# Pool mixer: group product on the residual itself with tokens as outputs, norm factor at PSUM eviction, running means as band products

## The reference, cut

```python
def rmsnorm(x, g):
    return x * lax.rsqrt(jnp.mean(x * x, axis=-1, keepdims=True) + NORM_EPS) * g

def pool_mixer(h, w_group, scale):            # h: (1, 528, 1024), groups of 256 channels
    hf = h.reshape(B, L, 4, 256)
    csum = jnp.cumsum(hf, axis=1)
    for g, w in enumerate((2, 4, 8, 16)):     # running mean over the last w tokens
        prev = jnp.pad(csum[:, :L - w, g, :], ((0, 0), (w, 0), (0, 0)))
        means.append((csum[:, :, g, :] - prev) / jnp.minimum(t, w))   # t = 1 .. L
    mixed = jnp.stack(means, axis=2) - hf
    return jnp.einsum('blgc,gcd->blgd', mixed, w_group).reshape(B, L, 1024) * scale

h = h + rmsnorm(f, norm_ffn_post[0])          # end of layer 0; f is the FFN's output
m = pool_mixer(rmsnorm(h, norm_mix_pre[1]), pool_w_group, pool_scale)
h = h + rmsnorm(m, norm_mix_post[1])
f = conv_ffn(rmsnorm(h, norm_ffn_pre[1]), ...)          # layer 1's FFN follows
```

## Time and profile before

| | |
|---|---|
| median of 3 runs | 2167.58 us (2165.72 to 2169.86) |
| the profiled execution, its own time | 2169.56 us |
| its span in the trace | 2167.8 us (1.76 us lie around it) |
| mean granted TensorE clock | 0.969 of full speed |
| PE busy | 2012.0 us (93%) |
| weight loads on PE | 1824.2 us (84%) |
| DVE, ACT, POOL busy | 958.1, 945.6, 870.7 us |

### The profile page before, as it was taken

The page is one execution under the profiler, slowest core; times in us unless marked ns, Lnnn a source line. Parts: engine busy times, 40 slices in busy tenths (PEclk is TensorE's granted clock), DMA queues, the critical chain, the costliest instruction groups (busy, mean ns, idle before and its releaser), DMA issues.

```text
span 2167.8 us, 36602 instructions
## 1 busy us (share of the span) xinstructions
PE 2012.0 (93%) x13518; PEld 1824.2 (84%) x13522; DVE 958.1 (44%) x1823; ACT 945.6 (44%) x1663; POOL 870.7 (40%) x530
## 2 busy tenths in 40 slices
PE   8999889998999999989888989999999479999997
PEld 6887668888877778989788979999998379999996
DVE  6874870227533230257688164334101864334102
ACT  3123762323644342155577355545423355555322
POOL 1444213442434444324433153443443733443443
PEclk7999999999999999989999999999999789999999
DMA  9641012231222333222100112222331003222332
GB/s 351 242 165 39 11 37 96 92 97 40 88 97 78 106 97 107 69 69 88 50 0 0 40 50 97 94 90 87 98 100 66 20 26 101 96 88 86 107 101 75
DMA packets 55529, 186.49 MB, mean 86 GB/s; under 512 B 7056, under 2 KB 10384, under 8 KB 55440
## 3 DMA queue, kind: packets, MB, share of 16 engines
q1 hardware_dynamic: 53600, 183.07, 25.0%
q10 hardware_dynamic: 1840, 2.19, 0.3%
HBM read 183.13 MB, written 2.10 MB: 85 GB/s over the span
## 4 chain that ended last, share of the span: by engine, by line
PE 82%; DVE 11%; ACT 3%; issue 2%; POOL 1%; DVEq 0%; DMA 0%; ACTq 0%; POOLq 0%
PE PS L686 68%; PE PS L895 2%; PE PS L974 2%; PE PS L853 1%; PE PS L928 1%; DVE work L2718 1%; PE PS L809 1%; DVE pool_s L411 1%; PE PS L870 1%; POOL X L1490 1%; DVE ada_acc L2261 1%; DVE small L2412 1%; PE PS L1052 1%; PE PS L1040 1%; PE PS L1327 1%
## 5 line engine op out<-in xcount | busy, mean ns | idle before, releaser
L1375 POOL TENSOR_TENSOR w_lo<-w_raw,w_hi 128x1024 fp32r<-128x1024 f32 x273 | 661.2, 2429 | 956.7 <-ACT w_hi L1568 956.5
L686 PE MATMUL PS<-H_hi,w_lo 128*128 128x256 f32 (+3 forms) x2184 | 596.0, 322 | 62.0 <-POOL H_lo L1530 26.6
L1568 ACT ACTIVATE w_hi<-w_raw 128x1024 fp32r<-128x1024 f32 (+2 forms) x317 | 307.9, 986 | 689.8 <-PE PS L686 642.0
L686 PE MATMUL PS<-H_lo,w_hi 128*128 128x256 f32 (+3 forms) x2184 | 587.7, 318 | 0.0
L686 PE MATMUL PS<-H_hi,w_hi 128*128 128x256 f32 (+3 forms) x2184 | 586.5, 317 | 0.0
L686 PEld LDWEIGHTS PS<-H_hi,w_lo 128*128 128x128 f32 x2184 | 375.5, 193 | 103.8 <-issue 51.4
L686 PEld LDWEIGHTS PS<-H_hi,w_hi 128*128 128x128 f32 x2184 | 376.0, 193 | 26.0
L686 PEld LDWEIGHTS PS<-H_lo,w_hi 128*128 128x128 f32 x2184 | 376.2, 193 | 24.7
L2718 DVE SCALAR_TENSOR_TENSOR work<-PS,vec,work 128x512 f32<-128x512 f32 (+4 forms) x264 | 187.0, 751 | 450.2 <-ACT work L1868 440.6
L686 PE MATMUL PS<-mid_hi,w_lo 128*128 128x256 f32 (+2 forms) x968 | 228.6, 294 | 3.6 <-DVE work L2718 3.6
L686 PE MATMUL PS<-mid_hi,w_hi 128*128 128x256 f32 (+2 forms) x968 | 226.9, 292 | 0.0
(11 more groups left out here) (334 smaller groups left out, 3053.7 us busy)
## 6 DMA issues: line engine op xcount, KB each, us to landing
w_raw<-stream SPq DMA_DIRECT2D x293, 512.0 KB, 3.7
ada_w<-ada SPq DMA_DIRECT2D x48, 512.0 KB, 6.4
X<-xT SPq DMA_DIRECT2D x8, 256.0 KB, 5.8
yT<-X SPq DMA_DIRECT2D x16, 128.0 KB, 1.7
rel_raw<-rel ACTq DMA_DIRECT2D x4, 256.0 KB, 2.6
vec<-vecs ACTq DMA_DIRECT2D x1, 390.0 KB, 3.8
sin_t<-rope ACTq DMA_DIRECT2D x1, 264.0 KB, 3.8
cos_t<-rope ACTq DMA_DIRECT2D x1, 132.0 KB, 2.4
```

Source lines behind the costliest of these rows:

```text
L686: last = pe.matmul(out[:, c0 + a:c0 + b], w, x[:, a:b], start=start and i == 0, stop=stop and i == 2)
L1375: gp.tensor_tensor(w_lo[:, o], w_raw[:, o], w_hi[:, o].bitcast(F32), ALU.subtract)\
L1568: return act_.activation(out, in_, ACT.Copy, scale=scale)
```

## The change

The group product no longer waits for the norm and the running means. By linearity, mean(norm(x) g) W is done as band * (r * (x (gW))), where r is a factor for each token:

- The gain goes into the weights: `upper_pool` on ACT scales the four 128 x 256 pieces of a pool block in place, then rounds it.
- `H_hi` and `H_lo` are made from `X` itself (`round_x` on ACT, `lower_x` on DVE).
- `pool_tiles(s)` on PE has tokens as outputs: 128 (or 16) tokens of `H` are the stationary operand, 256 columns of weights move. Half 0 has three token tiles (16, 128 and 128 tokens), half 1 two: 72 and 48 matmuls.
- `pool_norms(s)` gives the sums of squares for each token on its own partition: 24 and 16 float32 matmuls of 128 columns, where `sum_x_squares("down_b", s)` is dropped. The root (`root_pool`) works on 3 or 2 columns.
- `take_z` on ACT evicts a token tile with the root as a scale for each partition (`z_hi`, 1024 columns), `lower_z` on DVE makes `z_lo` from PSUM and `z_hi`.
- `pool_half(s)` on PE then multiplies `z` with a band matrix (1/w on w diagonals, less the identity) and gives the transposed layout back: 70 matmuls for half 0 (16 of 144, 16 of 128 and 38 of 16 columns) and 48 for half 1 (128, 144 and 16 columns, 16 of each, in part). `make_bands` builds the bands with 25 small DVE instructions after up_b; the band is waited for in ACT's `take_first("down_b")` before its weight splits, and by PE.
- `pooled_dve`, `pooled_gp`, `lower_gp` and `round_pooled` are gone. On POOL the first pool block's `w_lo` stands ahead of the residual's adds.

The diff, cut:

```diff
+POOL_TILES = (((0, META), (META, P), (META + P, P)), ((HALF2, P), (HALF2 + P, P)))
...
+            def pool_tiles(s):
+                first = 3 * s
                 for b in range(2):
...
+                    for i, (t0, tn) in enumerate(POOL_TILES[s], first):
+                        z = z_psum(i)
...
+                        for kk in range(4):
+                            kt = 4 * b + kk
+                            if i == first:
+                                pe.wait_ge(hh_ok[s], KD + kt + 1)
+                            xs = slice(kt * S2 + t0, kt * S2 + t0 + tn)
+                            ws = slice(slot * BLK + kk * 256, slot * BLK + (kk + 1) * 256)
+                            o = b * 512 + kk // 2 * 256
+                            for j, (l, r) in enumerate(((H_lo, w_hi), (H_hi, w_lo), (H_hi, w_hi))):
+                                last = pe.matmul(PS[0:tn, z, o:o + 256], l[:, xs], r[:, ws],
+                                                 start=kk % 2 == 0 and j == 0, stop=kk % 2 == 1 and j == 2)
...
+                    elif b == 0:
+                        sum_squares("down_b", 1)
+            def pool_norms(s):
+                for k in range(KD):
+                    pe.wait_ge(sqx_ok[s], TAIL_N["down_b"] * KD + k + 1)
+                    for i, (t0, _) in enumerate(POOL_TILES[s]):
+                        o = 512 * s + i * P
+                        last = pe.matmul(PS[:, 0, o:o + P], sqp[:, k * S2 + t0:k * S2 + t0 + P], ones[:, :],
+                                         start=k == 0 and i == 0, stop=k == KD - 1, skip_group_check=True)
+                last.then_inc(sum_ok[s], 1)
+            def pool_half(s):
+                pe.wait_ge(band_ok, 1)
+                pe.wait_ge(zl_ok, 5 if s else 3)
+                for m in range(8):
...
+                    g = m // 2
+                    out = PS[:, m % 4, COL2:]
+                    if s == 0:
+                        parts = ((1, META, P, 0, BAND), (2, META + P, P, 0, P), (0, 16, META, 16, 32))
+                    else:
+                        parts = ((2, HALF2, P, P, BAND), (3, HALF2, P, 0, BAND), (4, HALF2 + P, P, 0, P))
+                    for i, (tile, t0, rows_, a, b) in enumerate(parts):
+                        for t in (z_lo, z_hi):
+                            last = pe.matmul(out[:, t0:t0 + b - a], z_tile(t, tile, m)[0:rows_], band(g)[0:rows_, a:b],
+                                             start=i == 0 and t is z_lo, stop=s == 1 and i == 2 and t is z_hi,
+                                             skip_group_check=True)
...
-            sum_x_squares("down_b", 0)
-            sum_squares("down_b", 1)
+            pool_tiles(0)
+            pool_norms(0)
             pool_half(0)
             sum_squares("pool", 0)
-            sum_x_squares("down_b", 1)
+            pool_tiles(1)
+            pool_norms(1)
             sum_x_squares("pool", 0)
             pool_half(1)
             sum_squares("pool", 1)
...
+                if name == "down_b":
+                    act_.wait_ge(band_ok, 1)
                 cnt_["four"] += 1
...
+                for kk in range(4):
+                    w = w_raw[:, slot * BLK + kk * 256:slot * BLK + (kk + 1) * 256]
+                    chain.done(copy(w, w, v1("mix_pre", KD + 4 * b + kk)))
...
+            def take_z(s):
+                act_.wait_ge(rs2_ok[s], 4)
+                for i, (_, tn) in enumerate(POOL_TILES[s], 3 * s):
...
+                    copy(z_tile(z_hi, i)[0:tn], PS[0:tn, z_psum(i), :], zroot(i)[0:tn]).then_inc(zh_ok, 1)
...
-            next_upper("down_b", 0)
-            square_x("down_b", 0)
-            next_upper("down_b", 1)
+            upper_pool(0)
+            upper_pool(1)
+            for k in range(KD):
+                round_x(0, k)
+                if k >= 2:
+                    square_pool(0, k - 2)
+            square_pool(0, 6)
+            square_pool(0, 7)
+            take_half("down_b", 1)
+            root(1, 3)
             next_upper("down_b", 2)
-            take_half("down_b", 1)
-            root(0, 4)
-            root(1, 3)
+            root_pool(0)
+            take_z(0)
             next_upper("down_b", 3)
-            round_pooled(0)
+            for k in range(KD):
+                round_x(1, k)
             take_half("pool", 0, range(0, 4), "pool_scale")
             take_half("pool", 0, range(4, 8), "pool_scale")
             root(0, 5)
-            square_x("down_b", 1)
-            root(1, 4)
+            for k in range(KD):
+                square_pool(1, k)
+            root_pool(1)
             square_x("pool", 0)
-            round_pooled(1)
+            take_z(1)
...
+            def make_bands():
...
+                v.wait_ge(midl_ok, 2 * KF + 1)
...
+                chain.done(v.tensor_copy(ones_of(0)[:, 16:16 + P], ident[:, :]))
+                for g in range(4):
+                    w = POOLS[g]
+                    chain.wait()
+                    chain.done(v.tensor_tensor(ones_of(g + 1)[:, 16:], ones_of(g)[:, 16:],
+                                               ones_of(g)[:, 16 - w // 2:wide - w // 2], ALU.add))
+                    chain.wait()
+                    chain.done(v.scalar_tensor_tensor(band(g), ones_of(g + 1)[:, 16:], 1.0 / w, ones_of(0)[:, 16:],
+                                                      ALU.mult, ALU.subtract))
...
+            def lower_z(s):
+                for i, (_, tn) in enumerate(POOL_TILES[s], 3 * s):
+                    v.wait_ge(zh_ok, i + 1)
+                    v.scalar_tensor_tensor(z_tile(z_lo, i)[0:tn], PS[0:tn, z_psum(i), :], zroot(i)[0:tn],
+                                           z_tile(z_hi, i)[0:tn].bitcast(F32), ALU.mult, ALU.subtract)\
+                        .then_inc(zl_ok, 1)
...
+            make_bands()
             add_four(2)
             root(0, 3)
+            for k in range(KD + 2):
+                if k < KD:
+                    weigh("down_b", 0, "ffn_post", 0, k)
+                if k >= 2:
+                    lower_x(0, k - 2)
...
-            pooled_dve(0)
...
             root(0, 5)
             for k in range(KD):
                 weigh("pool", 0, "mix_post", KD, k)
-            root(1, 4)
-            pooled_dve(1)
-            before_up("pool", "mix_post", KD, KD + len(POOL_DVE), 2 * KD, KD)
+            root_pool(1)
+            lower_z(1)
+            before_up("pool", "mix_post", KD, 2 * KD, 2 * KD, KD)
```

268 lines of the change are left out of this document (124 added, 144 removed).

## The result

The change made the kernel a little slower: 2172.57 us (median of 12 runs) against 2167.88 (12 runs), a ratio of 1.0022 with an interval of 1.0013 to 1.0031. Forecast were 2155.1 and a gain of 12.5; measured is a loss of 4.7 us, and 2172.57 lies above the range's end of 2168.

What follows compares the result with a forecast made beforehand. PE was taken to bound the kernel outside a few stages, the vector engines this stage. First half -0.3 and second -13.85 sum to -14.15; with +1.65 taken back, -12.5, giving 2155.1 us; range 2147 to 2168.

Steps and rivals of the forecast that it cites:

- rival C: z eviction: DVE's `z_lo` contends with POOL and waits it out, +6 us, 2161 in all; chance 0.08.
- Bands: 70 x 0.115 ... of which the first part runs at the half level, +1.9: First half's band products on PE: 8.1 us, plus 1.9 for a first part at the half clock level.
- 0.5 of half clock: Second half's band products on PE: 0.5 us added for the half level, beside 5.5 for 48 products.
- a sum of -14.15: Pool stage, both halves: -0.3 us in the first and -13.85 in the second, before the reserve.
- D: Rival: TensorE's half clock level stretches the stage's tile products, norms and bands; slower, 2171.6 us; chance 0.10.
- B: Rival: short products cost more, the 118 band products 0.18 us rather than 0.115, +7.7, 2162.8; chance 0.12.
- E: Rival: new chain of norms, root, z, bands as long in the second half too, or bands late; 2165 to 2169; chance 0.08.
- The reserve of 1.65: Pool stage, both halves: +1.65 us taken back from the summed gain for waits and the clock.

Runs made afterwards that it cites:

- e12: Changed kernel with all 70 first-half band products moving 256 columns, 38 of them still at 16 rows, no fillers: 2176.84 us, 1.0043 of before.
- e15: Changed kernel with all 70 first-half band products at 128 rows and 256 columns, no fillers: stage 95.19 us, kernel 2169.23 us (one execution).
- e17: Changed kernel with all 118 band products at 128 rows and 256 columns, unread products in all five waits: 2158.16 us, 0.9951 of before.
- e1: Changed kernel with 48 unread 256-column products between the norm sums and the first half's band products: 2170.57 us, 1.0008 of before.
- e4: Changed kernel with 48 unread products ahead of the first half's bands and more in the other five waits: 2165.88 us, 1.0 of before.
- e8: Changed kernel with the 38 first-half band products of 16 rows given 128 rows, left at 16 columns, no fillers: 2169.11 us.

## Why the prediction was wrong

**What held.** What bounds the kernel in this stage was read rightly, and the forecast's times up to z were close. The last tile of `X` was 17.7 us after the stage's start (17.8 forecast), the norms took 5.52 (5.3), and the root and z of the first half 6.0 (6.2). The second half's bands could start 16.0 us after the sums (16.2). DVE and ACT in the changed kernel, where the bands are built, and `z_lo` of both halves:

```profile
1549.18 0.17 DVE L2899 TENSOR_TENSOR lnw_r<-work,lnw_r 128x16 fp32r<-128x16 f32 x1
...
1549.39 2.96 ACT L1556 ACTIVATE w_hi<-w_raw 128x1024 fp32r<-128x1024 f32 x3 [6.68 <-DVE lnw_r L2899]
...
1692.84 3.65 DVE L2926 SCALAR_TENSOR_TENSOR z_lo<-PS,st,z_hi 16x1024 fp32r<-16x1024 f32 x3 [1.25 <-ACT z_hi L1556]
...
1736.18 2.48 DVE L2926 SCALAR_TENSOR_TENSOR z_lo<-PS,st,z_hi 128x1024 fp32r<-128x1024 f32 x2 [2.37 <-ACT z_hi L1556]
```

The bands were ready 8.0 us after the last `mid_lo` (5 to 8 forecast), ACT waited 6.68 us for them and PE not at all. `z_lo` took 1.22 and 1.24 us against 1.3, so rival C (contention) didn't come about. POOL had nothing to do at either place, so the rule that a DVE instruction with one SBUF input doesn't wait for POOL (the Trainium skill, "SBUF — State Buffer", section "Who interferes with whom") was not put to the test by these rows.

**The step that failed** is the term "Bands: 70 x 0.115 ... of which the first part runs at the half level, +1.9", and its twin in the second half, "0.5 of half clock". I took it from the first four tiles of before, whose clock was back after 3.7 us, and carried it to the whole of a pass of other products. Even the rows did not say that: the 0.72 from 1700 to 1712 is a second set of products at 1.2 GHz from end to end, and I counted only the first. Measured: 20.0 us from the first band product to the sums instead of 11.5, and 10.8 instead of 7.7 in the second half. The forecast had also left the sums behind each pass at their price of before; they start at the low clock now, 6.13 and 6.48 against 3.93 and 3.72, +5.0 together. And `sum_squares(down_b,1)` ran in part at the half level ahead of all that and ended 24.2 us after the stage's start (22.6 forecast): the bands started 1.9 us later than forecast. 8.5 + 3.1 + 5.0 + 1.9 = 18.5 on a sum of -14.15 is +4.35; the stage showed +3.9.

**The rivals.** D had the cause and the sign, with a chance of 0.10, and its own sign came true: the clock from 1700 to 1740 is 0.74, under the 0.75 it named. That its time was near (2171.6 against 2172.57) is in part luck: it spread the half level over tile products, norms and bands, but the tile products (0.12 us apart) and the norms (1.00) ran at the full clock, while the bands lost 11.6 us and the sums behind them, which it left out, 5.0. What spoke for it was in the text: a stage whose products were at 0.76 already, and a pass of scattered short pieces. I discounted it because waits got shorter, and that isn't what decided. B's sign came true as well, products 0.245 us apart where it named 0.15, but not its cause: at the full clock the band products are 0.113 (from 1738.76 to 1741.35 in the second half) to 0.14 us apart; 0.21 to 0.25 is their price at the half level. E expected a new chain as long as the old; it wasn't, as the times up to z show. The Trainium skill ("TensorE: Matmul & The Clock Gate", section "Part 1: The HAM clock gate") says that the slow level is the default and activity releases it. The trace agrees with the default, but being busy by the profile did not release it here: 0.50 over 20 us in which PE was busy for 17.34, and e12 was busier than e15 and stayed low.

**The sum at the full clock.** e17 gives -10.3 in the stage. Against -14.15, 1.9 of the rest is the bands' later start in the first half (40.3 us after the stage's start against 38.4), 0.9 the pass (12.45 against 11.5) and 1.0 the second half (24.9 against 23.9). The reserve of 1.65 for waits and the clock was 2.2 too small even there.

## What to carry to other kernels

When work moves to TensorE as many short products, price them at both clock levels, and ask whether anything hides the low one: in this kernel the old products were at the low clock for long, too, and fillers ahead of them gained nothing, because DVE's last tiles set when the first four could be evicted. Read the clock of every set of products from its own window, not from the first set alone. Look for products that use few of the 128 rows, or few columns, in a pass of their own behind a wait: merging them, giving them full rows with zeros, and filling the waits with unread products took the same algorithm from 1.0022 to 0.997 of the kernel before. What follows such a pass counts too, since it starts at the clock that the pass leaves.

## What the runs showed that I had not expected

- Making products bigger made a pass faster. 70 products of 128 rows and 256 columns: 13.3 us; the same with 128 to 144 columns: 18.1; 38 of them at 16 rows and 256 columns: 22.5.
- A stream of warm products can fall to 1.2 GHz without any wait of its own: in e1 the pass starts at the prices of the full level, and from 1701.61 on it is at those of the half level, ahead of its first wait. Products of 128 rows and 256 columns can fall too: before, at 1745.28, 0.8 us after a wait of 2.22 us.
- The float32 norm sums of 128 columns held 1.00 for 5.52 us, with records 0.112 apart, right behind tile products at the full clock. The fp32r band products of up to 144 columns fell from it in e1's first pass and held it in e4's second. Why was not tried.
- Changing between stationary operands of 128 and 16 rows costs a step of 0.34 and 0.29 us at the low clock against 0.21 without (in the trace of after from 1697.27 to 1697.61 and from 1698.27 to 1698.56). With 128 rows in all (e8) the first eight products take 1.70 us instead of 1.96.
